# Reordering the mixer's three branches, cutting up the opening panel of the attention's output projection, and four buffers for the modulation pieces

## The reference

```python
# first block: the gated mixer with three branches
a = silu(layernorm(conv31(a_val * sigmoid(a_gate)) + b)) @ w_a_out
p = einsum('bsgc,gco->bsgo', multiscale_pool_minus_token(u_pool), w_pool_grp) * pool_scale
c = (c_b * conv3(c_c * c_x)) @ w_c_out
merged = gates[0] * a + gates[1] * p + gates[2] * c
x = x + merged @ w_o
# then cross attention, a mixture of 16 experts, and the second block, of two layers:
mod = silu(c) @ w_ada[i] + b_ada[i]          # six modulation vectors of a layer
x = x + g1 * (sparse_attention(h) @ nsa_w_out)     # first layer (diff attention in the second)
x = x + g2 * (relu(h @ w_mlp_in[i])**2 @ w_mlp_out[i])
```

## Time and profile before

| | before |
|---|---|
| time of 3 runs | 1381.13, 1380.66, 1378.83 us; median 1380.66 |
| profiled execution | 1378.08 us, span 1376.4 us |
| PE busy | 1328.1 us (96%) |
| DVE busy | 952.2 us (69%) |
| ACT busy | 658.0 us (48%) |
| mean granted TensorE clock | 0.989 of full |
| HBM read | 256.77 MB, 187 GB/s over the span |

### The profile page before, as it was taken

One profiled execution on the slowest core, in us unless ns is written; L12 is line 12 of the kernel. 1 busy time (PEld: TensorE's weight loads), 2 busy tenths in 40 slices (PEclk: granted clock), 3 DMA queues, 4 the chain that ended last, 5 costly groups with the idle time before them and its releaser, 6 DMA issues.

```text
span 1376.4 us, 25619 instructions
## 1 busy us (share of the span) xinstructions
PE 1328.1 (96%) x10729; PEld 1269.4 (92%) x10729; DVE 952.2 (69%) x1212; ACT 658.0 (48%) x861; POOL 79.1 (6%) x131
## 2 busy tenths in 40 slices
PE   7999999898999999999999999899999998999998
PEld 7999999898899999999989578899999876999998
DVE  4679886754677777776775868777778866655443
ACT  4544435354443333333557736444456445555442
POOL 4022000000000000011100000000000000000000
PEclk9999999999999999999999999999999999999999
DMA  8665635344278888886451035888884512356551
GB/s 229 201 219 177 197 113 178 128 154 137 94 254 282 271 276 263 276 265 205 138 183 62 1 132 191 290 306 312 317 278 140 188 62 62 123 184 214 183 184 62
DMA packets 172602, 259.11 MB, mean 188 GB/s; under 512 B 5141, under 2 KB 147778, under 8 KB 172514
## 3 DMA queue, kind: packets, MB, share of 16 engines
q1 hardware_dynamic: 160906, 203.13, 45.3%
q0 software_dynamic: 10768, 53.43, 11.1%
q10 hardware_dynamic: 840, 1.28, 0.3%
HBM read 256.77 MB, written 1.05 MB: 187 GB/s over the span
## 4 chain that ended last, share of the span: by engine, by line
PE 80%; DVE 10%; DMA 4%; ACT 4%; issue 2%; SPq 0%; ACTq 0%; DVEq 0%
PE ring L693 56%; PE acc L693 23%; DVE w_lo L1953 2%; ACT w_hi L1425 2%; DMA raw<-in_w_in_dram 2%; DMA raw<-in_w_mlp_in_dram 2%; DVE arena L2136 1%; ACT arena L1425 1%; DVE arena L2002 1%; PE acc L1235 1%; PE ring L1052 1%; DMA raw<-in_w_xo_dram 1%; DVE arena L2363 1%; DMA raw<-in_w_o_dram 0%; ACT h_hi L1425 0%
## 5 line engine op out<-in xcount | busy, mean ns | idle before, releaser
L1953 DVE TENSOR_TENSOR w_lo<-raw,w_hi 128x2048 fp32r<-128x2048 f32 (+1 forms) x191 | 436.4, 2288 | 241.8 <-ACT w_hi L1425 241.2
L693 PE MATMUL ring<-h_hi,w_hi 128*128 128x256 f32 (+1 forms) x2024 | 577.7, 285 | 4.4 <-DVE w_lo L1953 1.8
L693 PE MATMUL ring<-h_hi,w_lo 128*128 128x256 f32 (+1 forms) x2024 | 572.3, 283 | 0.0
L693 PE MATMUL ring<-h_lo,w_hi 128*128 128x256 f32 (+1 forms) x2024 | 570.7, 282 | 0.0
L1425 ACT ACTIVATE w_hi<-raw 128x2048 fp32r<-128x2048 f32 (+1 forms) x191 | 364.0, 1906 | 258.8 <-DMA raw<-in_w_mlp_out_dram 74.8
L693 PEld LDWEIGHTS ring<-h_hi,w_hi 128*128 128x128 f32 x2024 | 383.3, 189 | 9.7 <-issue 4.0
L693 PEld LDWEIGHTS ring<-h_lo,w_hi 128*128 128x128 f32 x2024 | 384.2, 190 | 2.6 <-issue 2.2
L693 PEld LDWEIGHTS ring<-h_hi,w_lo 128*128 128x128 f32 x2024 | 384.4, 190 | 0.0
L693 PE MATMUL acc<-e_hi,w_hi 128*128 128x256 f32 x768 | 217.1, 283 | 0.5 <-DVE e_lo L2656 0.4
L693 PE MATMUL acc<-e_lo,w_hi 128*128 128x256 f32 x768 | 215.4, 281 | 0.0
L693 PE MATMUL acc<-e_hi,w_lo 128*128 128x256 f32 x768 | 215.3, 280 | 0.0
(11 more groups left out here) (315 smaller groups left out, 1380.4 us busy)
## 6 DMA issues: line engine op xcount, KB each, us to landing
arena<-in_w_ada_dram POOLq DMA_DIRECT2D x64, 768.0 KB, 5.8
raw<-in_w_mlp_in_dram SPq DMA_DIRECT2D x32, 1024.0 KB, 5.5
raw<-in_w_mlp_out_dram SPq DMA_DIRECT2D x32, 1024.0 KB, 5.4
raw<-in_w_in_dram SPq DMA_DIRECT2D x24, 1024.0 KB, 5.2
raw<-in_w_e_gate_dram SPq DMA_DIRECT2D x16, 1024.0 KB, 5.4
raw<-in_w_e_up_dram SPq DMA_DIRECT2D x16, 1024.0 KB, 6.4
raw<-in_w_e_down_dram SPq DMA_DIRECT2D x16, 1024.0 KB, 5.7
raw<-in_diff_w_in_dram SPq DMA_DIRECT2D x12, 1024.0 KB, 5.1
```

Of the source, the lines that this page charges most:

```text
L693: return nc.tensor.matmul(dst, lhs, rhs, start=start, stop=stop, **kw)
L1953: tt(w_lo[q % SPL][:, 0:n], raw[q % RAW][:, 0:n], w_hi[q % SPL][:, 0:n].bitcast(F32), ALU.subtract)\
```

## The change

Five things at once. (1) `pool_out` moves ahead of `a_out` in the plan, on PE and in the split operands (pooling now in `h_hi[0:4]`, `a_out` in `h_hi[4:8]`), and it adds up in `acc` instead of ring banks. DVE gates the pooling branch and adds it to `c_out` (`rest`) before `a_out` is taken, and merges pair by pair as `a_out` drains. (2) ACT's splits ahead of the four roundings end at `w_o` 2; DVE splits `w_o` 0 after the pooling pairs and `w_o` 1 inside `done("a_out", 0)`. (3) `keep_busy` shrinks from 10 to 2. (4) `first_blocks` runs `n_o` 0 in three parts, k outermost: blocks 0 to 2 before the transposes of unit 15, blocks 3 and 4 before `n_values(15)`, blocks 5 to 7 behind it. (5) The modulation pieces get four buffers; the first two of the second layer wait for `cmp_made` 2, the third for `no_ready` 4; `V_CMP` moves to block 16 and its copy waits for `n_keys_doubled`. `pairs_ready` waits at two more blocks.

```diff
     add("c_out", [cols(a["w_c_out"][0], i * 512, 512) for i in range(2)])
+    add("pool_out", [a["w_pool_grp"][0].rearrange("g c o -> c g o")])
     add("a_out", [cols(a["w_a_out"][0], i * 512, 512) for i in range(2)])
-    add("pool_out", [a["w_pool_grp"][0].rearrange("g c o -> c g o")])
...
-        P_CMP, PT_CMP, N_P, N_PT, V_CMP, K_CMP, HID_C = 34, 38, 42, 48, 54, 46, 65
+        P_CMP, PT_CMP, N_P, N_PT, V_CMP, K_CMP, HID_C = 34, 38, 42, 48, 16, 46, 65
...
+        def ada_piece(n):
+            return flat((ADA_RAW, ADA_RAW + 6, 12, 18)[n % 4], 0, ADA_W)
...
-                if g >= 2:
-
-                    pool.wait_ge(S("ada_used"), turn.at("piece", g - 1))
-                pool.dma_start(flat(ADA_RAW, (n % 2) * ADA_W, ADA_W), src).then_inc(S(f"ada_landed{n % 2}"), 16)
+                if g >= 4:
+
+                    pool.wait_ge(S("ada_used"), turn.at("piece", g - 3))
+                if g == 34:
+                    pool.wait_ge(*sig("no_ready", 4))
+                pool.dma_start(ada_piece(n), src).then_inc(S(f"ada_landed{n % 4}"), 16)
...
-            pool.wait_ge(*sig("no_ready", 4))
+            pool.wait_ge(S("cmp_made"), 2)
...
+            def first_blocks(p, f, blocks, ready):
+
+                if blocks[0] == 0:
+                    open_panel(p)
+                    open_fill(f)
+                wh = w_hi[p % SPL][:].rearrange("p (k n) -> p k n", k=KB)
+                wl = w_lo[p % SPL][:].rearrange("p (k n) -> p k n", k=KB)
+                for k in blocks:
+                    ready(k)
+                    for b in range(2):
+                        o, c = bank(f)[:, b * T:(b + 1) * T], slice(b * P, (b + 1) * P)
+                        mm(o, wh[:, k, c], h_hi[:, k, :], k == 0 and b == 0, False, skip_group_check=True)
+                        mm(o, wh[:, k, c], h_lo[:, k, :], False, False, skip_group_check=True)
+                        last = mm(o, wl[:, k, c], h_hi[:, k, :], False, k == KB - 1, skip_group_check=True)
+                if blocks[-1] == KB - 1:
+                    last.then_inc(S("panel_done"), 1)
...
-            pe.wait_ge(S("a_split"), 1)
-            for i in range(2):
-                linear(PN["a_out"] + i, FL["a_out"] + 2 * i, 4, 4, lambda k: h_hi[:, k, :], lambda k: h_lo[:, k, :])
-
             pe.wait_ge(S("p_split"), 1)
             p = PN["pool_out"]
             open_panel(p)
             for g in range(4):
-                f = FL["pool_out"] + g
-                open_fill(f)
                 for b in range(2):
                     c = slice(g * 256 + b * P, g * 256 + (b + 1) * P)
-                    o = bank(f)[:, b * T:(b + 1) * T]
-                    mm(o, w_hi[p % SPL][:, c], h_hi[:, 4 + g, :], True, False)
-                    mm(o, w_hi[p % SPL][:, c], h_lo[:, 4 + g, :], False, False)
-                    last = mm(o, w_lo[p % SPL][:, c], h_hi[:, 4 + g, :], False, True)
+                    o = acc[g][:, b * T:(b + 1) * T]
+                    mm(o, w_hi[p % SPL][:, c], h_hi[:, g, :], True, False)
+                    mm(o, w_hi[p % SPL][:, c], h_lo[:, g, :], False, False)
+                    last = mm(o, w_lo[p % SPL][:, c], h_hi[:, g, :], False, True)
             last.then_inc(S("panel_done"), 1)
-            keep_busy(FL["w_o"], 10)
+            pe.wait_ge(S("a_split"), 1)
+            for i in range(2):
+                linear(PN["a_out"] + i, FL["a_out"] + 2 * i, 4, 4, lambda k: h_hi[:, 4 + k, :], lambda k: h_lo[:, 4 + k, :])
+
+            keep_busy(FL["w_o"], 2)
             full("w_o", h_ready("merged_ready"), norm="x", raw=True)
...
-                    if k % 2 == 0:
+                    if k in (0, 2, 3, 4, 5, 6):
...
+                if u == HEADS - 1:
+                    first_blocks(PN["n_o"], FL["n_o"], range(0, 3), pairs_ready("no_ready"))
...
+            first_blocks(PN["n_o"], FL["n_o"], range(3, 5), pairs_ready("no_ready"))
             n_values(HEADS - 1)
-            full("n_o", pairs_ready("no_ready"), norm="m0", raw=True)
+            first_blocks(PN["n_o"], FL["n_o"], range(5, KB), pairs_ready("no_ready"))
+            for i in range(1, 4):
+                if i < 3:
+                    linear(PN["n_o"] + i, FL["n_o"] + i, KB, 2, lambda k: h_hi[:, k, :], lambda k: h_lo[:, k, :])
+                else:
+                    linear_last("m0", PN["n_o"] + i, FL["n_o"] + i)
+                stat_pair("m0", i - 1)
...
+            act.wait_ge(S("p_done"), 1)
+            func(h_hi[:, 0:4, :], u_pad[:, :, 16:16 + T], ACT.Copy).then_inc(S("p_hi"), 1)
             act.wait_ge(S("a_silu"), 4)
-            func(h_hi[:, 0:4, :], blk(CX, 4), ACT.Copy).then_inc(S("a_hi"), 1)
-            act.wait_ge(S("p_done"), 1)
-            func(h_hi[:, 4:8, :], u_pad[:, :, 16:16 + T], ACT.Copy).then_inc(S("p_hi"), 1)
-            ahead(PN["w_o"])
+            func(h_hi[:, 4:8, :], blk(CX, 4), ACT.Copy).then_inc(S("a_hi"), 1)
+            ahead(PN["a_out"] + 1)
             for j in range(4):
...
+            dve.wait_ge(S("p_hi"), 1)
+            tt(h_lo[:, 0:4, :], u_pad[:, :, 16:16 + T], h_hi[:, 0:4, :].bitcast(F32), ALU.subtract).then_inc(S("p_split"), 1)
             dve.wait_ge(S("a_hi"), 1)
-            tt(h_lo[:, 0:4, :], blk(CX, 4), h_hi[:, 0:4, :].bitcast(F32), ALU.subtract).then_inc(S("a_split"), 1)
-            dve.wait_ge(S("p_hi"), 1)
-            tt(h_lo[:, 4:8, :], u_pad[:, :, 16:16 + T], h_hi[:, 4:8, :].bitcast(F32), ALU.subtract).then_inc(S("p_split"), 1)
...
-            for i in range(4):
-                f = FL["a_out"] + i
-                done("a_out", i // 2)
-                drains(tt(m[:, 2 * i:2 * i + 2].rearrange("p b t -> p (b t)"), bank(f)[:], flat(GATES, i * 512, 512), ALU.mult), f)
-            for i in range(4):
-                drained_wait(dve, FL["c_out"] + i)
-                drained_wait(dve, FL["a_out"] + i)
-            chain.did(tt(m, m, blk(GATES + 16, 8), ALU.add))
...
+            rest = blk(GATES + 16, 8)
             for i in range(4):
-                f = FL["pool_out"] + i
                 g = blk(GATES + 8, 8)
                 for b in (2 * i, 2 * i + 1):
-                    last = stt(g[:, b], bank(f)[:, (b % 2) * T:(b % 2 + 1) * T], vcol("pool_s", b), g[:, b], ALU.mult, ALU.mult)
-                drains(last, f)
+                    chain.did(stt(g[:, b], acc[i][:, (b % 2) * T:(b % 2 + 1) * T], vcol("pool_s", b), g[:, b], ALU.mult, ALU.mult))
+                chain.settle()
+                drained_wait(dve, FL["c_out"] + i)
+                s = slice(2 * i, 2 * i + 2)
+                chain.did(tt(rest[:, s], rest[:, s], g[:, s], ALU.add))
+            ahead(PN["pool_out"])
+            for i in range(4):
+                f = FL["a_out"] + i
+                if i == 2:
+                    merged_low(1)
+                    dve.wait_ge(S("panel_done"), PN["a_out"] + 2)
+                else:
+                    done("a_out", 0)
+                s = slice(2 * i, 2 * i + 2)
+                drains(tt(m[:, s].rearrange("p b t -> p (b t)"), bank(f)[:], flat(GATES, i * 512, 512), ALU.mult), f)
                 drained_wait(dve, f)
                 chain.settle()
-                s = slice(2 * i, 2 * i + 2)
-                tt(m[:, s], m[:, s], g[:, s], ALU.add).then_inc(S("merged"), 1)
-                if i:
+                tt(m[:, s], m[:, s], rest[:, s], ALU.add).then_inc(S("merged"), 1)
+                if i in (1, 3):
                     merged_low(i - 1)
             merged_low(3)
             ahead(PN["w_o"])
...
+            dve.wait_ge(S("n_keys_doubled"), 2)
             drains(nc.vector.tensor_copy(blk(V_CMP)[:, 0], bank(f)[:, 0:T]), f)
```

More of the change, by code:

```diff
@@ L240, in fill_plan @@
                     ("c_x", 2), ("c_c", 2), ("c_b", 2), ("u_pool", 2), ("gates", 12), ("x_k", 4), ("ln_stat", 1), ("x_v", 2), ("lv_stat", 1),
-                    ("x_v2", 2), ("c_out", 4), ("a_out", 4), ("pool_out", 4), ("w_o", 4), ("x_stat", 1),
+                    ("x_v2", 2), ("c_out", 4), ("a_out", 4), ("w_o", 4), ("x_stat", 1),
                     ("x_q", 2), ("x_s0", 1), ("x_q2", 1), ("x_s1", 1), ("x_t0", 1), ("x_q3", 1), ("x_att", 2 * X_HEADS - 3), ("x_o", 4), ("ffn_stat", 1), ("router", 1),
@@ L2170, in _ @@
             ahead(PN["x_v"] + 3)
+            dve.wait_ge(S("p_hi"), 1)
+            tt(h_lo[:, 0:4, :], u_pad[:, :, 16:16 + T], h_hi[:, 0:4, :].bitcast(F32), ALU.subtract).then_inc(S("p_split"), 1)
             dve.wait_ge(S("a_hi"), 1)
-            tt(h_lo[:, 0:4, :], blk(CX, 4), h_hi[:, 0:4, :].bitcast(F32), ALU.subtract).then_inc(S("a_split"), 1)
-            dve.wait_ge(S("p_hi"), 1)
-            tt(h_lo[:, 4:8, :], u_pad[:, :, 16:16 + T], h_hi[:, 4:8, :].bitcast(F32), ALU.subtract).then_inc(S("p_split"), 1)
+            tt(h_lo[:, 4:8, :], blk(CX, 4), h_hi[:, 4:8, :].bitcast(F32), ALU.subtract).then_inc(S("a_split"), 1)
             m = blk(MERGED, 8)
@@ L2351, in ada @@
                 g = 32 * l + n
-                land = g // 2 + 1
-                dve.wait_ge(S(f"ada_landed{n % 2}"), 16 * land if turn.reg is None
```

(6 more changed lines are left out.)

## The result

| | before | changed |
|---|---|---|
| median of 12 runs | 1379.34 us (1375.37 to 1381.27) | 1383.8 us (1378.6 to 1388.32) |
| profiled execution, its span | 1378.08, 1376.4 us | 1380.36, 1378.7 us |
| mean granted clock of it | 0.989 | 0.986 |

The changed kernel is slower: ratio 1.0035, 95% interval 1.0023 to 1.0047, which is 4.8 us (3.2 to 6.5). The two profiled executions differ by only 2.3 us. Runs of one kernel scatter by more than that, so what follows compares stretches of several profiles, not two spans.

A forecast was written before the change was run, and what follows sets the result against it. The prediction took the kernel as bound by the chain that ended last, 80% of it on PE. Merge -0.3, cut panel +3.6 and buffers +0.3 gave +3.6 on 1380.66, so 1384.3 us, range 1377.8 to 1387.0.

The forecast's parts named there:

- The sum: Whole kernel: merge -0.3, cut panel +3.6, buffers +0.3, together +3.6 us, giving 1384.3 us; main case, chance 0.57.
- They push `n_values(15)` back by their own length: End of the attention: 30 `n_o` 0 matmuls with no gap to fill delay `n_values(15)` by 3.6 us (1.8 to 6.4).
- `out_lo(3)` is upstream of everything for 70 us: End of the attention: the chain runs through `out_lo(3)`, splits and MLP panel load to 881.24 us, so all moves by 3.6.
- And PE's own work there is not: Same 70 us stretch behind `out_lo(3)`: PE's own matmuls are not upstream of what follows; no size given.
- At 881 PE's wait grows from 5.9 to some 9.5: Transposes of L1052: PE's wait for DVE's modulation pieces grows from 5.9 to some 9.5 us.
- The sign at `out_lo(3)`: End of the attention: if the forecast is right, `out_lo(3)` comes 3 to 4 us later after its neighbours.
- Blocks 6 and 7 now also wait, 0.6 us: Last blocks of `n_o` 0: PE stalls 0.6 us for rounding and subtracting, off the chain, counting nothing.
- One load has taken the place of another: Mixer's merge: ACT's roundings wait for `w_o` 2 instead of `w_o` 3; -0.3 us (-2.2 to +0.8).
- Four buffers: Modulation pieces: removed DVE waits save nothing, one load sent sooner crowds the MLP panel; +0.3 us (0 to 0.9).
- Swallowed: Rival, behind `out_lo(3)`: DVE's chain has slack, only PE's 0.6 us stall stays; +0.3 us, 1381.0; chance 0.21.
- The prefetch that thins the traffic: Rival, MLP's second panel: fewer pieces in its way, landing in 5.4 us; -4.7 us, 1376.0; chance 0.12.
- The clock that stays down: Rival, end of the attention: all 30 matmuls run at half clock; +6.4 us, 1387.1; chance 0.10.

The follow-up runs named there:

- only_blocks: Kernel before with only the cut opening panel of `n_o` (part 4 of the change); +5.2 us (2.6 to 7.9) against the kernel before.
- blocks_in_gap: Kernel before with `n_o` 0's blocks 0 to 2 in PE's 2.0 us wait, blocks 3 to 7 behind `n_values(15)`; -4.1 us against the kernel before.
- after_splits_early: Changed kernel with the splits of `n_o` 2 and 3 moved ahead of `out_lo(3)`; -0.6 us (-2.8 to 1.8) against the kernel before.
- only_merge: Kernel before with only the mixer's part (parts 1 to 3 of the change); 0.0 us (-1.8 to 1.9) against the kernel before.
- only_buffers: Kernel before with only the four modulation-piece buffers (part 5 of the change); +0.8 us (-1.9 to 3.4) against the kernel before.
- hold_pieces: Kernel before with the four buffers, the second layer's piece 4 held until the MLP's second panel landed; -0.3 us against the kernel before.
- the combined one: Changed kernel with `n_o` 0's blocks 0 to 2 in PE's wait, `w_o` splits later in the merge, pieces 6 and 7 earlier; -5.0 us against before.

## Why the prediction was right, and where not

*The sum* (+3.6, 1384.3 us) came out as +4.8 (3.2 to 6.5), 1383.8 us, and for the reason given. That the two times lie only 0.5 us apart is in part luck: the prediction set out from 1380.66, the median of three runs, where twelve have 1379.34, and its difference was 1.2 us too small. By itself the cut panel measures 5.2 (3.6 forecast), the merge 0.0 (-0.3) and the buffers 0.8 (0.3).

*"They push `n_values(15)` back by their own length"*: right. 3.6 us forecast, 3.8 at one clock, +3.7 by the medians of *only_blocks*. In the two profiles of the cut panel in which the clock fell, lo2-lo3 is 13.34 and 14.86 us, against 10.98 without the cut. That the gap lies one unit earlier decided it, as *blocks_in_gap* shows.

*"`out_lo(3)` is upstream of everything for 70 us"*: right for the queue behind it, shown by *after_splits_early*. *"And PE's own work there is not"* holds only by a margin: freed of the two panels, the chain runs over PE's 168 matmuls behind `out_lo(3)`, and is 4.6 us shorter.

*"At 881 PE's wait grows from 5.9 to some 9.5"*: wrong. The wait stayed at 5.8, and "no longer than 6" was one of the prediction's own signs of being wrong. The step assumed that PE's arrival at the transposes stays where it was. But PE's list hangs on `out_lo(3)` as well, through the last blocks of `n_o` 0 and through the panels behind it: PE gets there 64.3 us after `out_lo(3)` before and 64.2 in the changed kernel (the start of the transposes less the wait). So the delay moves both sides and does not show in the wait, which was 5.1 to 7.6 in the profiles that still have it, with no link to `first_blocks` (5.7 in *only_merge*, 6.2 in *only_blocks*). The sign at `out_lo(3)`, 3 to 4 us later, does not show in the pair of profiles that it was meant for either (0.8), because of the clock; at one clock it does (3.8).

*"Blocks 6 and 7 now also wait, 0.6 us"*: right, 0.5 for `h_lo`, off the chain.

*"One load has taken the place of another"*: right; the rounding of `w_o` 2 ended at 250.2 (251 forecast) with the merged pairs behind it. Its size, -0.3, was taken against a profile in which the old merge had lost the clock. In five other profiles of the old merge the stretch is 56.3 to 57.1 us, not 58.7, and with the changed merge 58.3 to 58.9: some +2 in those profiles, beyond the bound of +0.8, where the time of *only_merge* shows 0.0 (-1.8 to 1.9). The two are just compatible at about +1.9. That PE would be at half clock behind the pause was right; that it would cost no more than before was not. Whether the shorter `keep_busy` or the pause itself does it was not tried.

*Four buffers, +0.3*: 0.8 (-1.9 to 3.4), with the panel at 13.6 us in *only_buffers* and 13.25 in the changed kernel. The waits removed from DVE gave nothing, as forecast; no run shows the term of 0.3 for the load sent out sooner by itself, as the interval is wider than it.

*The rivals.* Swallowed: excluded, by *only_blocks* and by the 3.9 us still there at the end of the MLP. The prefetch that thins the traffic: the panel landed in 13.25 us, not 7.3; and *hold_pieces* shows that even a panel made faster hands the crowd on. The clock that stays down: the 30 matmuls ran at full clock in the changed kernel and in *only_blocks*; in *after_splits_early* 18 of them took 3.86 us instead of 2.33, so it does happen, in one of the four profiles that have them in this place.

## What to carry to other kernels

Fill the gap, not its neighbourhood: thirty of these matmuls one unit behind PE's wait cost 3.8 us, while eighteen of them inside it cost nothing and kept the clock up, and that kernel ran 4.1 us (1.8 to 6.3) faster. Before work is put in front of the last operand of a stage, look at what queues behind that operand on the other engines, because moving those splits ahead was worth some 5 us, in the changed kernel (+4.8 to -0.6) and in the combined one (-5.0 to -10.1). And a faster piece in a row of loads only names the next late load: three times here (`w_o` 2, `w_o` 3, the MLP's panels) the gain had to be followed one step further.

## What the runs showed of the chip that was not expected

The same PE instructions with the same 2.0 us wait ran lo2-lo3 in 10.98 or 10.99 us in four profiles, 9.56 in one and 7.98 or 7.99 in two: PE's clock fell behind that wait in some executions and not in others. The window of *only_merge* above has it at 1.00; the same window of *only_buffers*, with 21 matmuls in place of 36:

```profile
802.00:806.00 4.00, 4.00 (x21) 2.20 (x18) 1.05 (x3) 0.49 (x1) 0.00 (x0) 0.50 0.00 0
```

What decides between the two stays open. With the gap filled it stayed up in both profiles that fill it without adding splits (8.06 and 8.07). One such fall is worth 3.0 us, nearly the size of the whole effect, so a pair of profiles is read at one clock or not at all.
